# A two-layer hybrid encoder step: the norms' squares summed on VectorE, four dense weight buffers, new banks for w_o

## The reference

```python
for l in range(2):
    sh1, sc1, g1, sh2, sc2, g2 = split(silu(c) @ ada_w[l] + ada_b[l], 6)   # adaLN vectors
    h = rms(x, norm1_w[l]) * (1 + sc1) + sh1
    y = mixers(h) @ w_o[l]            # gated recurrence and latent attention, side by side
    x = x + g1 * y
    h = rms(x, norm2_w[l]) * (1 + sc2) + sh2
    if l == 0: f = (silu(h @ w_gate) * (h @ w_up)) @ w_down                # dense, width 2816
    else:      f = sum over the top 2 of 8 experts of the same, width 3584
    x = x + g2 * f
```

## Time and profile before

| what | value |
|---|---|
| time, median of 3 runs (lowest, highest) | 1759.36 us (1759.02, 1760.96) |
| the profiled execution's own time | 1758.77 us |
| its span in the trace | 1756.9 us |
| PE busy, share of the span | 1641.1 us, 93% |
| DVE busy | 1282.2 us, 73% |
| ACT busy | 1068.2 us, 61% |
| mean granted clock of TensorE | 0.974 |
| loads of expert weights | 336 of 1 MB |

### The profile page before, as it was taken

The page is one execution under the profiler, slowest core; times in us unless marked ns, Lnnn a source line. Parts: engine busy times, 40 slices in busy tenths (PEclk is TensorE's granted clock), DMA queues, the critical chain, the costliest instruction groups (busy, mean ns, idle before and its releaser), DMA issues.

```text
span 1756.9 us, 26847 instructions
## 1 busy us (share of the span) xinstructions
PE 1641.1 (93%) x9270; PEld 1361.3 (77%) x9270; DVE 1282.2 (73%) x1482; ACT 1068.2 (61%) x1311; POOL 108.3 (6%) x101
## 2 busy tenths in 40 slices
PE   6998988999989987769999999999999999999994
PEld 3885677999979756648888888888888888888883
DVE  3467445554455845569889899889899898989885
ACT  4455434444355644537777777777777777777772
POOL 0031010000002200000000010000000000100000
PEclk9999999999999999879999999999999999999998
DMA  9852454445446052469999999999999999999992
GB/s 387 310 202 109 170 183 151 165 159 191 156 164 235 25 208 89 171 227 378 374 360 378 367 375 377 364 387 369 366 395 372 367 384 361 374 374 367 385 375 101
DMA packets 111405, 494.17 MB, mean 281 GB/s; under 512 B 8049, under 2 KB 8353, under 8 KB 98929
## 3 DMA queue, kind: packets, MB, share of 16 engines
q1 hardware_dynamic: 107136, 479.60, 72.9%
q0 software_dynamic: 3840, 12.57, 1.9%
q10 hardware_dynamic: 368, 1.19, 0.2%
HBM read 484.97 MB, written 8.35 MB: 281 GB/s over the span
## 4 chain that ended last, share of the span: by engine, by line
PE 85%; DVE 8%; ACT 3%; issue 2%; DMA 2%; DVEq 0%; SPq 0%; ACTq 0%; POOLq 0%
PE bank L1176 18%; PE bank L1144 11%; PE bank L1145 11%; PE bank L1148 11%; PE bank L638 8%; PE bank L640 7%; PE bank L639 7%; PE bank L674 2%; PE bank L1161 1%; DVE w_lo L2282 1%; DMA ring<-w_ada 1%; DVE wd_lo L2282 1%; DVE wm_lo L1701 1%; PE bank L821 1%; PE bank L653 1%
## 5 line engine op out<-in xcount | busy, mean ns | idle before, releaser
L2282 DVE TENSOR_TENSOR w_lo<-xring,w_hi 128x2048 fp32r<-128x2048 f32 x224 | 513.1, 2291 | 77.3 <-ACT w_hi L1592 67.0
L1592 ACT ACTIVATE w_hi<-xring 128x2048 fp32r<-128x2048 f32 x224 | 428.2, 1912 | 5.3 <-PE bank L1148 5.3
L1144 PE MATMUL bank<-w_hi,hg_hi 128*128 128x512 f32 x896 | 362.6, 405 | 0.6 <-DVE hg_lo L2287 0.6
L1145 PE MATMUL bank<-w_hi,hg_lo 128*128 128x512 f32 x896 | 350.7, 391 | 0.0
L2282 DVE TENSOR_TENSOR wd_lo<-xring,wd_hi 128x2048 fp32r<-128x2048 f32 x112 | 256.6, 2291 | 16.8 <-ACT wd_hi L1592 16.5
L1592 ACT ACTIVATE wd_hi<-xring 128x2048 fp32r<-128x2048 f32 x112 | 214.9, 1919 | 58.9 <-PE bank L1176 58.6
L1148 PE MATMUL bank<-w_lo,hg_hi 128*128 128x512 f32 x896 | 240.9, 391 | 0.0
L1148 PEld LDWEIGHTS bank<-w_lo,hg_hi 128*128 128x128 f32 x896 | 168.6, 188 | 35.7 <-DVE w_lo L2282 0.5
L1144 PEld LDWEIGHTS bank<-w_hi,hg_hi 128*128 128x128 f32 x896 | 168.8, 188 | 33.5 <-DVE hg_lo L2287 1.0
L1145 PEld LDWEIGHTS bank<-w_hi,hg_lo 128*128 128x128 f32 x896 | 169.3, 189 | 31.5
L638 PE MATMUL bank<-hm_hi,wm_hi 128*128 128x288 f32 x448 | 140.2, 313 | 26.5 <-DVE misc L1690 6.6
(11 more groups left out here) (332 smaller groups left out, 2550.1 us busy)
## 6 DMA issues: line engine op xcount, KB each, us to landing
xring<-w_moe SPq DMA_DIRECT2D x336, 1024.0 KB, 7.0
ring<-w_ada SPq DMA_DIRECT2D x32, 1536.0 KB, 8.0
ring<-w_win SPq DMA_DIRECT2D x22, 1024.0 KB, 5.5
ring<-w_up SPq DMA_DIRECT2D x22, 1024.0 KB, 4.7
ring<-w_down SPq DMA_DIRECT2D x8, 1408.0 KB, 6.0
ring<-w_wo SPq DMA_DIRECT2D x8, 1024.0 KB, 5.0
ring<-w_wqb SPq DMA_DIRECT2D x2, 1152.0 KB, 5.8
ring<-w_wkvb SPq DMA_DIRECT2D x2, 1024.0 KB, 5.5
```

The lines of the kernel that those rows point to most:

```text
L1144: mm(banks[r % 2][:, :], hg_hi[:, k], part(w_hi, k), start=k == 0, stop=False)
L1145: mm(banks[r % 2][:, :], hg_lo[:, k], part(w_hi, k), start=False, stop=False)
L1592: A(w_hi[:, p] if p < 2 else wd_hi[:, r % 2], xpiece[:, r % 2, p], ACT.Copy).then_inc(sem("hi_done"), 1)
L2282: v.tensor_tensor(lo, xpiece[:, r % 2, p], hi.bitcast(F32), ALU.subtract).then_inc(sem("lo_done"), 1)
```

## The change

1. `add_squares` is new on DVE: the squared slices of three norms (second norm of layer 0, first and second of layer 1) are added into the first slice, seven additions a norm, and PE sums one slice with one matmul. Five additions stand in DVE's queue ahead of the last `add_gated`, two behind it.
2. `wf_hi` and `wf_lo` have four buffers. The two pieces of the first "up" are rounded by ACT ahead of the squares and finished by DVE ahead of the last `add_gated`; the second "up" follows directly after the last `shift_rest`; in the loops each piece is prepared one double piece (four pieces in "down": two more) earlier. For layer 1's first norm, the first two tiles are rounded and finished in the same way at the end of the dense layer; the third stays where it was.
3. The dense tiles are laid out anew, so that these buffers don't overlap what is in use at that time.
4. The first two w_o tiles use banks 0 and 7, the others 1 to 6; `modulation_sums(("att", l, 6))` moves ahead of the third tile's `weights_rest` and of `keep_rows(2)`.
5. In the mixers, the rotation of queries ("rotq", 0) goes ahead of the chunk products (3, 4, 5) on PE, and on DVE `rotate(0)` and `norm_k(0)` go ahead of parts of `form_states`.
6. One slab of `ada_w` moves from the first attention place of layer 1 to a place "r1" behind the square sum of the last norm, and is turned at "r2" ahead of the rank product; the gate vector's transpose waits for its sum (`gains_ready`). Layer 1's stream of loads ends with this slab, and the first expert loads wait until PE has read it.

The diff, cut to its core:

```diff
-ADA_AT.update({("att", 1, i): 1 for i in range(5)})
-ADA_AT.update({(name, l): 1 for name, l in (("n2a", 0), ("n2b", 0), ("n1a", 1), ("n1b", 1))})
-ADA_FLUSH = (("start", 0), ("att", 0, 6), ("n2c", 0), ("att", 1, 6))
+ADA_AT.update({("att", 1, i): 1 for i in range(1, 5)})
+ADA_AT.update({(name, l): 1 for name, l in (("n2a", 0), ("n2b", 0), ("n1a", 1), ("n1b", 1), ("r1", 1))})
+ADA_FLUSH = (("start", 0), ("att", 0, 6), ("n2c", 0), ("att", 1, 6), ("r2", 1))
...
-             ("q", 5), ("ss", "q4"), ("v", 1), ("k", 0), ("ss", "q5"), ("u", (3, 4, 5)), ("rotq", 0), ("k", 1), ("ss", "k0"),
+             ("q", 5), ("ss", "q4"), ("v", 1), ("k", 0), ("ss", "q5"), ("rotq", 0), ("u", (3, 4, 5)), ("k", 1), ("ss", "k0"),
...
-                    use(("wo", l, k), 6 + k)
+                    use(("wo", l, k), 7 * k)
...
-            use(("wo", l, k), k - 2)
+            use(("wo", l, k), k - 1)
...
-        wf_hi = tiles(sb("wf_hi", 2 * D, F32R)[:, :], 2)
-        wf_lo = tiles(sb("wf_lo", 2 * D, F32R)[:, :], 2)
+        wf_hi = tiles(sb("wf_hi", 4 * D, F32R)[:, :], 4)
+        wf_lo = tiles(sb("wf_lo", 4 * D, F32R)[:, :], 4)
+        aT_hi = sb("aT_hi", NF * T, F32R)
+        sb("below_h", 16640 - 8 * D - NF * T)
         h_hi, h_lo = sb("h_hi", KD * T, F32R), sb("h_lo", KD * T, F32R)
-        aT_hi, aT_lo = sb("aT_hi", NF * T, F32R), sb("aT_lo", NF * T, F32R)
+        aT_lo = sb("aT_lo", NF * T, F32R)
...
+            sp.wait_ge(*used_up(len(STREAM) - 2))
             sp.wait_ge(*used_up(len(STREAM) - 1))
             sp.sem_inc(sem("lo_done"), 6)
...
+                norm = 2 * l + (name == "n2")
+                if norm:
+                    pe.wait_ge(sem("squares_added"), (KD - 1) * norm)
+                    full(mm(o[:, 0:T], ones, sq8_f[:, 0:T], start=True, stop=True), ("ss", l, name))
+                    return
...
                 sum_x_squares(l, "n2")
+                modulation(("r1", l) if l else ("n2b", l))
...
+            modulation(("r2", 1))
             o = use(("rank",))
...
-                for j in range(3):
+                for j in range(2 if l else 0, 3):
                     round_weights((NP + KD) * l + j)
...
+                    for u in range(2):
+                        round_up_piece(0, 0, u)
                 square_x(l, "n2", (sem("x1_ready"), KD * l))
...
-                    for u in range(2):
-                        round_up_piece(0, 0, u)
                     for k in range(KD):
                         act.wait_ge(sem("h2_scaled"), k + 1)
                         shift_rounded(0, h_hi, 24, k, "h2_rounded")
+                    for u in range(2):
+                        round_up_piece(0, 1, u)
                     modulation_rows(("n2b", l))
...
+                    for j in range(2):
+                        round_weights(NP + KD + j)
...
+            modulation_rows(("r1", 1))
             take(act, ("logits", "by expert"))
...
+            def add_squares(before, k):
+                dve.wait_ge(sem("x_squared"), KD * (before + 1) + k + 1)
+                v.tensor_tensor(sq8_f[:, 0:T], sq8_f[:, 0:T], sq8_f[:, k * T:(k + 1) * T], ALU.add
+                                ).then_inc(sem("squares_added"), 1)
+                dve.wait_ge(sem("squares_added"), (KD - 1) * before + k)
...
-                form_states((3, 4, 5))
                 rotate(0)
+                form_states((3, 4))
                 norm_k(0)
+                form_states((5,))
                 rotate(1)
...
                 scale_weighed(2)
+                modulation_sums(("att", l, 6))
                 weights_rest((NP + KD) * l + NP + 2)
                 keep_rows(2)
-                modulation_sums(("att", l, 6))
...
+                    if k == KD - 1:
+                        if l == 0:
+                            for u in range(2):
+                                up_piece_rest(0, 0, u)
+                        for i in range(1, KD - 2):
+                            add_squares(2 * l, i)
                     add_gated(l, ("wo", l, k), k, 16, "x1_ready")
+                for i in range(KD - 2, KD):
+                    add_squares(2 * l, i)
...
+                        if d == KD * DOWN_PIECES - 1:
+                            for j in range(2):
+                                weights_rest(NP + KD + j)
+                            for i in range(1, KD - 2):
+                                add_squares(1, i)
...
             dve.sem_inc(sem("chosen_ready"), 1)
+            modulation_sums(("r2", 1))
+            dve.sem_inc(sem("gains_ready"), 1)
```

More of the change, by code:

```diff
@@ L151 @@
     STREAM += [("wo", _l, j, 2048) for j in range(4)]
-    if _l == 0:
+    if _l:
+        STREAM += [("ada", 0, n, 3072) for n in ada_slabs(("r1", 1))]
+    else:
         STREAM += [("ada", 0, n, 3072) for place in ("n2a", "n2b") for n in ada_slabs((place, 0))]
@@ L290, in psum_plan @@
         else:
+            ada(("r1", l), (7, None))
             at[0] = 0
@@ L1022, in _ @@
                 sum_x_squares(l, "n2")
+                modulation(("r1", l) if l else ("n2b", l))
                 if l == 0:
-                    modulation(("n2b", l))
                     for b in range(2):
@@ L1071, in _ @@
                                 c = 128 * (f - 8 * p)
-                                w = [x[:, n % 2, c:c + 128] for x in (wf_hi, wf_lo)]
+                                w = [x[:, n % 4, c:c + 128] for x in (wf_hi, wf_lo)]
                                 last = three(o[:, 0:T], w, aT_hi[:, f * T:(f + 1) * T], aT_lo[:, f * T:(f + 1) * T],
@@ L1507, in _, with round_up_piece @@
                     round_weights((NP + KD) * l + NP + k)
+                if l == 0:
+                    def round_up_piece(q, j, u):
+                        s = slot_of(POS["up", 0, 0] + j) * SLOTW + u * D
+                        act.wait_ge(slot_full[slot_of(POS["up", 0, 0] + j)], q * 16 + fills(POS["up", 0, 0] + j))
+                        A(wf_hi[:, 2 * (j % 2) + u], ring[:, s:s + D], ACT.Copy).then_inc(sem("ffn_hi"), 1)
+                    for u in range(2):
+                        round_up_piece(0, 0, u)
                 square_x(l, "n2", (sem("x1_ready"), KD * l))
@@ L1513, in _ @@
                     nc.scalar.preload_act_table_set("silu_and_others")
-                    def round_up_piece(q, j, u):
-                        s = slot_of(POS["up", 0, 0] + j) * SLOTW + u * D
-                        act.wait_ge(slot_full[slot_of(POS["up", 0, 0] + j)], q * 16 + fills(POS["up", 0, 0] + j))
-                        A(wf_hi[:, u], ring[:, s:s + D], ACT.Copy).then_inc(sem("ffn_hi"), 1)
                     def round_down_piece(d):
-                        use_, count = piece_done(2 * NF + d - 2)
+                        use_, count = piece_done(2 * NF + d - 4)
                         if use_:
@@ L1529, in round_down_piece @@
                         act.wait_ge(slot_full[slot_of(at)], fills(at))
-                        A(wf_hi[:, d % 2, 0:n], ring[:, slot_of(at) * SLOTW + c:slot_of(at) * SLOTW + c + n], ACT.Copy
+                        A(wf_hi[:, d % 4, 0:n], ring[:, slot_of(at) * SLOTW + c:slot_of(at) * SLOTW + c + n], ACT.Copy
                           ).then_inc(sem("ffn_hi"), 1)
@@ L1553, in _ @@
                         for j in range(NSLOT):
-                            hidden(q, j, lambda u: round_up_piece(q, j + 1, u))
+                            hidden(q, j, lambda u: round_up_piece(q, j + 2, u))
                     q = NF // NSLOT
                     for j in range(NF % NSLOT):
-                        hidden(q, j, (lambda u: round_up_piece(q, j + 1, u)) if j < NF % NSLOT - 1 else round_down_piece)
-                    for d in range(2, KD * DOWN_PIECES):
+                        hidden(q, j, lambda u: round_down_piece(2 * j + u))
+                    for d in range(4, KD * DOWN_PIECES):
                         round_down_piece(d)
+                    for j in range(2):
+                        round_weights(NP + KD + j)
             for k in range(KD):
@@ L2092, in _, with up_piece_rest @@
                     dve.sem_inc(sem("om_split"), 1)
+                def up_piece_rest(q, j, u):
+                    s = slot_of(POS["up", 0, 0] + j) * SLOTW + u * D
+                    dve.wait_ge(sem("ffn_hi"), q * (2 * NSLOT) + (2 * j + u + 1))
+                    b = 2 * (j % 2) + u
+                    v.tensor_tensor(wf_lo[:, b], ring[:, s:s + D], wf_hi[:, b].bitcast(F32), ALU.subtract
+                                ).then_inc(sem("ffn_lo"), 1)
                 for k in range(KD):
@@ L2103, in _ @@
                     dve.sem_inc(sem("a_split"), 2)
-                    def up_piece_rest(q, j, u):
-                        s = slot_of(POS["up", 0, 0] + j) * SLOTW + u * D
-                        dve.wait_ge(sem("ffn_hi"), q * (2 * NSLOT) + (2 * j + u + 1))
-                        v.tensor_tensor(wf_lo[:, u], ring[:, s:s + D], wf_hi[:, u].bitcast(F32), ALU.subtract
-                                        ).then_inc(sem("ffn_lo"), 1)
```

(8 more changed lines are left out.)

24 lines of the change are left out of this document (14 added, 10 removed).

## The result

The changed kernel takes 1728.93 us (median of four runs, 1726.84 to 1731.33), the kernel before 1760.16 beside it: a ratio of 0.9822, with a 95% interval of 0.9807 to 0.9838. The forecast was 1730 within 1723 to 1741, and faster. A later comparison, five runs against nine, gave 0.9839 (0.9824 to 0.9853), 1730.59 against 1759.28. The profiled execution took 1726.84, with a span of 1725.0; against the profile before that is 31.9 us less.

The account below looks back on a forecast made before the run. PE is busy throughout the expert loop, more than half the kernel and untouched, so gains lie at seams between stages. Terms sum to 29 us off 1758.77, giving 1729.8, stated as 1730, with 8 in 10 within 1723 to 1741.

Parts of the forecast that it names:

- Start of w_o: PE's stop before w_o ends sooner once the flushed turn's sum moves up DVE's queue: 6.2 us in layer 0, 5.65 in layer 1.
- if the clock stays up: After layer 0's shortened stop, the first half of w_o takes 2.9 us and ends at 230.5.
- the rival of the falling clock: Clock falls despite shorter stops: w_o wins 2.2 less, two slice passes lose 3.5 each; 9 lost, 1739 us; chance 0.12.
- Second norm of layer 0: One-slice square sum and pieces prepared ahead win 4.5 us up to the second double piece, bounds 3 and 5.5.
- allowance of 1 us for the slab behind the roundings: Layer 0's second double piece: PE still turns a slab ACT copies behind two roundings, allowed 1 us, ending at 282.7.
- Down and layer 1's first norm: Four buffers end idle weight loads in "down": 2.2 us; layer 1's first norm and the pass behind it: 5.1 us.
- The cover at no cost: Layer 1's first norm: two rests and five additions cost nothing, their pieces being two ahead; without that cover, 1 us.
- Second norm of layer 1, mixers, slab: Wins of 1.6 us at the norm, 2.4 in both layers' mixers, 1.3 from the slab leaving layer 1's attention.
- The end: Sum at "r2" and later expert loads after the last norm cost nothing; 0.5 us lost if the sum is uncovered.
- Issue: Rival: PE waits for its own instructions, w_o starts no earlier, 11.85 us lost, time 1742; chance 0.05.
- the expert loop: Rival: the loop loses its rhythm; 0.26 us more per pair eats the 29 us, 0.3 gives 1764; chance 0.05.
- DVE as the bound at the norms: Rival: an addition with its wait costs 0.9 us, not 0.49; 6.5 lost, time 1737; chance 0.06.

Follow-up runs that it names:

- e1: Changed kernel with the flushed turn's sum moved back behind the third w_o tile's remainder and keep_rows(2) on VectorE, new banks kept: 1738.71 us.
- e3: Kernel before with only the flushed turn's sum moved right behind scale_weighed(2) in both layers, old banks kept: 1750.30 us against 1760.00.
- e5: Changed kernel run again with nothing altered: 1730.59 us.
- e8: Changed kernel with keep_rows(2) earlier, second norms' squares and additions between tiles, and a slab's copy and sum ahead of layer 0's second pair of dense pieces: 1722.14 us.
- e9: Changed kernel with only two of the four dense buffers used in the down stage: 1733.58 us.
- e11: Changed kernel with the first two dense pieces rounded behind layer 0's second norm again, ahead of the shifted slices: 1731.36 us.
- e2: Changed kernel with the old banks for w_o, the second norm's sum and the slabs around it, the flushed turn's sum keeping its new place: 1731.07 us.
- e6: Changed kernel with keep_rows(2) ahead of the third w_o tile's remainder on VectorE in both layers: 1728.26 us.
- e12: Kernel e8 with banks 6 and 7 exchanged from w_o on: 1720.31 us.

## Why the prediction was right, point by point

**Start of w_o.** Right in mechanism and size, 5.9 and 5.4 for 6.2 and 5.65, and shown by e1 and e3. Its step "if the clock stays up" is where luck lay. The first profile has the full clock behind layer 0's turn, but of nine profiles with the same two short stops eight have it slow for some us there (e5: 0.57). In these eight the rest of layer 0's w_o, from the second half of its first tiles on, takes 0.7 to 1.4 us longer than at the full clock (23.75 to 24.42 us, against 23.04, from its first product to its last). In layer 1 of the pair the slow clock took back 1.9. The prediction saw this rival in the first half of w_o and set its loss there at 2.2 for both layers. In the first half it came in only two of the 22 starts of w_o with the short stop ahead, both in layer 1, in e8 and here in e9:

```profile
665.40:668.60 3.20, 3.20 (x15) 3.20 (x15) 0.53 (x1) 2.47 (x6) 0.00 (x0) 0.50 0.90 323
```

So the rival of the falling clock is half right: it came mostly behind the stop that remained.

**Second norm of layer 0.** The step that was mis-sized: 3.8, not 4.5. The square sum won 0.6 (0.95 forecast), and the allowance of 1 us for the slab behind the roundings was 0.7 short, since its turn waits for a sum that stands behind two remainders on DVE. That the pieces delay the last `add_gated` by over 2 us was right, and e11 shows that this is nearly all they win.

**Down and layer 1's first norm.** 2.3 and 4.7 for 2.2 and 5.1. The cover at no cost was real: e9, which takes it away, pays 1.7.

**Second norm of layer 1, mixers, slab.** 1.2, 2.5 (1.28 and 1.26) and 1.7 for 1.6, 2.4 and 1.3: the first and the last within their bounds, the mixers a little above their upper bound of 2.4. No run puts the slab back, so its 1.7 rests on the pair of profiles alone, and so do the 1.9 that layer 1's first norm wins behind its Ln (4.7 in all, 2.85 by Ln), where ACT drops two roundings.

**The end.** The prediction put it at nothing, and nothing is lost: the moved slab and its sum hold no one up. But 3.0 us are won there, which no term of the sum had. In the pair they come with the clock: under the logits it is 0.66 before (727 to 731 us) and 1.00 after (696.5 to 701.5), under the rank product 0.50 before (736.6 to 740.8) and 1.00 after (706.8 to 709.1). It is hardly chance alone. From the last Ln to the first product of the expert loop the two profiles without the change take 43.0 us (before) and 43.1 (e3), and the twelve with it 40.2 to 42.0, e2 and e11 with their slow clock from 700 us on among them. So at least about 1 us seems to come with the change. That the moved slab, which gives PE work in this stretch, is the cause is not shown: no run tests it.

**The sum.** The terms give 27.6 for 29. The attention's clock (2.8), the end (3.0), the start (0.4) and w_o's loss in layer 1 (-1.9) make 31.9 of it in the profiles; in the medians of the two comparisons it is 31.2 and 28.7. So the forecast was right by its terms, which came out 1.4 short. That the total came out near 29 or above all the same is in part luck: a gain at the end that was not foreseen, and the clock.

**The rivals.** "Issue" was refuted by e1 to e3, the expert loop by its unchanged window, DVE as the bound at the norms by the additions' 0.48.

The rule of the Trainium skill, "TensorE: Matmul & The Clock Gate", section "Part 1: The HAM clock gate", by which activity releases the slow clock, agrees with what followed the long stops in e1 (a granted clock of 0.50 from 234 to 239 us, and full again from 240 on); but equal stops of 1.45 us were followed by either clock here, so for short ones the rows leave it open.

## What to carry to other kernels

When PE stops at a seam, look for the last instruction of another engine that ends within a tenth of a us of the restart, whatever releaser the row names, and ask what it stands behind in its queue: moving one short instruction up was worth more (9.7 us in e3) than any larger edit that a run undid. Work that is moved ahead of a norm pays only if the engine has room there; count its queue up to the last instruction that the norm needs. When a seam is closed, the next wait is a us or two behind it, and it can be closed by the same reading, as e6, e8 and e12 do.

## What the runs showed of the hardware

The granted clock differs between executions of one program, and the scatter of their times goes with it: of eleven runs of the kernel before in one session, that at 0.969 took 1763.59 us, those at 0.973 took 1757.30 and 1757.25. One profile is thus a sample: the clock in layer 0's attention was slow in four of eleven profiles of the same code, and in one of the two with the earlier code up to there (before, but not e3). In layer 0's w_o, with a second stop of 1.45 us it was slow behind it in eight of nine; without that stop (e6, e8, e12) in none of three. In layer 1 it was slow somewhere in w_o in those three as well, and in e5 it stayed full behind both short stops, for which these runs show no cause.
